# Mixer projections of a hybrid decoder: from one f32 product to three products of rounded parts

## The reference, cut to what matters

```
x += 1/2 * gate1 * SwiGLU(mod1(norm(x)))
h  = mod2(norm(x));  z = h @ W_in        # one projection for all mixer groups and branch gates
     A: u * (tril(W_s) v + b)            # spatial gating, columns ua, va
     B: forgetting attention, 8 heads    # qb, kb, vb, forget rows; paged cache for the samples
     C: mLSTM, 4 heads                   # qc, kc, vc, oc, input and forget rows
x += gate2 * W_out( sum_b sigmoid(g_b) * (y_b @ W_branch_b) )
x += 1/2 * gate3 * SwiGLU(mod3(norm(x)))
```

## Time and profile before

| | us |
|---|---|
| median of 3 runs | 3485.57 (3480.32 to 3488.34) |
| the profiled execution, its own time | 3474.84 |
| span of the profiled execution | 3473.1 |
| granted TensorE clock, mean | 0.971 |

### The profile page before, as it was taken

One profiled execution on the slowest core, in us unless ns is written; L12 is line 12 of the kernel. 1 busy time (PEld: TensorE's weight loads), 2 busy tenths in 40 slices (PEclk: granted clock), 3 DMA queues, 4 the chain that ended last, 5 costly groups with the idle time before them and its releaser, 6 DMA issues.

```text
span 3473.1 us, 49844 instructions
## 1 busy us (share of the span) xinstructions
PE 3302.7 (95%) x21518; PEld 2747.9 (79%) x21518; DVE 1053.2 (30%) x1901; ACT 705.1 (20%) x1072; POOL 138.0 (4%) x269
## 2 busy tenths in 40 slices
PE   6999999989899998999989999999898999989999
PEld 4999986656676687999979999865565767879999
DVE  3332340132531114333343333311334211143333
ACT  2221222120431002212122222121123210022121
POOL 0000000001102000000000000000021020000000
PEclk9999999989999999999999999999999999999999
DMA  5344431201228521232213333311021384112221
GB/s 225 146 156 169 153 120 50 85 25 34 90 79 279 178 103 57 114 138 105 110 73 139 153 146 128 129 74 61 25 72 57 118 272 158 73 73 86 85 89 72
DMA packets 115404, 390.53 MB, mean 112 GB/s; under 512 B 12416, under 2 KB 62944, under 8 KB 96880
## 3 DMA queue, kind: packets, MB, share of 16 engines
q1 hardware_dynamic: 97152, 338.36, 26.8%
q0 software_dynamic: 14432, 34.09, 2.8%
q10 hardware_dynamic: 3600, 14.89, 1.1%
HBM read 373.61 MB, written 13.69 MB: 112 GB/s over the span
## 4 chain that ended last, share of the span: by engine, by line
PE 85%; DVE 7%; DMA 4%; ACT 2%; SPq 1%; issue 1%; ACTq 0%; DVEq 0%
PE g L716 75%; PE tb L716 5%; PE q L716 4%; DMA w<-in_w_up 2%; DVE area L1933 2%; DMA area<-in_w_ada 1%; DMA area<-in_cache_v 1%; DVE area L1615 1%; DVE area L1845 1%; DVE w_lo L1658 1%; DVE h_lo L1627 1%; PE tb L719 1%; DVE area L1616 1%; ACT w_hi L1281 0%; DMA area<-in_cache_k 0%
## 5 line engine op out<-in xcount | busy, mean ns | idle before, releaser
L716 PE MATMUL g<-h_hi,w_hi 128*128 128x272 f32 x2816 | 590.4, 291 | 37.6 <-DVE h_lo L1627 24.7
L716 PE MATMUL g<-h,w 128*128 128x272 f32 x2304 | 570.1, 404 | 28.5 <-DVE area L1915 24.4
L716 PE MATMUL g<-h_lo,w_hi 128*128 128x272 f32 x2816 | 591.1, 291 | 0.0
L716 PE MATMUL g<-h_hi,w_lo 128*128 128x272 f32 x2816 | 584.5, 289 | 0.0
L716 PEld LDWEIGHTS g<-h,w 128*128 128x128 f32 x2304 | 443.1, 195 | 151.7 <-issue 32.7
L1281 ACT ACTIVATE w_hi<-w 128x1024 fp32r<-128x1024 f32 (+2 forms) x240 | 274.2, 1144 | 1262.7 <-PE g L716 935.8
L716 PEld LDWEIGHTS g<-h_hi,w_hi 128*128 128x128 f32 x2816 | 443.0, 190 | 59.5 <-ACT area L1295 27.7
L1658 DVE TENSOR_TENSOR w_lo<-w,w_hi 128x1024 fp32r<-128x1024 f32 (+2 forms) x240 | 319.3, 1332 | 509.7 <-ACT w_hi L1281 506.4
L716 PEld LDWEIGHTS g<-h_hi,w_lo 128*128 128x128 f32 x2816 | 448.5, 191 | 0.0
L716 PEld LDWEIGHTS g<-h_lo,w_hi 128*128 128x128 f32 x2816 | 447.0, 190 | 0.0
L716 PE MATMUL g<-area,w 128*128 128x272 f32 x1280 | 307.4, 395 | 3.4 <-DVE area L1919 2.6
(11 more groups left out here) (220 smaller groups left out, 2254.3 us busy)
## 6 DMA issues: line engine op xcount, KB each, us to landing
w<-in_w_up SPq DMA_DIRECT2D x44, 2048.0 KB, 8.1
w<-in_w_ada SPq DMA_DIRECT2D x32, 2048.0 KB, 8.2
w<-in_w_in SPq DMA_DIRECT2D x16, 2048.0 KB, 8.2
w<-in_w_down SPq DMA_DIRECT2D x16, 1536.0 KB, 7.3
w<-in_w_gate SPq DMA_DIRECT2D x48, 512.0 KB, 5.3
w<-in_w_down SPq DMA_DIRECT2D x16, 1280.0 KB, 5.8
area<-in_cache_k SPq DMA_DIRECT2D x72, 256.0 KB, 4.4
area<-in_cache_v SPq DMA_DIRECT2D x72, 256.0 KB, 4.2
```

Of the source, the lines that this page charges most:

```text
L716: return pe.matmul(o, a, b, start=start, stop=stop, skip_group_check=True, **kw)
```

## The change

The mixer's projections, the gate rows, the queries and keys and the branch gates become three products of rounded parts, as in the feed-forward. The branch products and the output product stay f32.

`norm` now splits the mixer's input too; the lower part `HX` lies in x's place. x is stored block by block as it comes ready, and loaded again in two halves after the last gate. Queries move to `YB`'s place and keys to a place of their own, `KB_`. Weights are split by pieces of 128x1024: 57 pieces a mixer, listed in `JOBS`. ACT rounds a piece into a place of `FIRST_HI`, `LATER_HI`, `VALUE_HI` or `WHM` (`hi_part`), DVE writes the lower part over the original in the slot (`lo_part`), and PE waits for the piece (`split_in`). Both are put by hand between the other steps of ACT's and DVE's programs; those of the fills hang on the half unit before (`next_job`).

Some waits move: the third page load of a layer (n == 2) waits for the sample scores and ACT's stores, the loads of the past forget values (POOL, line 684) for the end of vb, and the reload of x for the last gate.

```diff
+JOBS = [("ua", i) for i in range(4)] + [("va", i) for i in range(4)] + [("rows", 0)]
+JOBS += [(name, i) for name in ("qkc", "vc", "oc") for i in range(4)]
+JOBS += [("qk", i) for i in range(8)] + [("vb", i) for i in range(4)]
+JOBS += [("merge", i) for i in range(3 * KD)]
...
+def next_job(u):
+    what, _, h = FILLS[u]
+    kind, i = fill_job(u)
+    if h or what.startswith("branch") or (kind, i + 1) not in JOB:
+        return None
+    return kind, i + 1
...
                     if n == 2:
-                        sp.wait_ge(s_fd, 48 * l + 16)
+                        sp.wait_ge(s_ss, 2 * (l + 1))
+                        sp.wait_ge(s_outa, 16 * 11 * (l + 1))
...
-                        sp.wait_ge(s_ss, 2 * (l + 1))
-                        sp.wait_ge(s_outa, 16 * 11 * (l + 1))
-                        sp.wait_ge(s_xs, 16 * (l + 1))
-                        sp.dma_start(X[:], out["y"]).then_inc(s_xr, 16)
+                    if name == "out1":
+                        sp.wait_ge(s_xs, 128 * (l + 1))
+                        sp.wait_ge(s_fill, FILL_L * l + LAST_GATE + 1)
+                        for q in range(2):
+                            sp.dma_start(X[:, 4 * q:4 * q + 4, :], out["y"][:, 4 * q:4 * q + 4, :]).then_inc(s_xr[q], 16)
...
+            def split_in(l, job):
+                pe.wait_ge(s_ml, len(JOBS) * l + JOB[job] + 1)
+                return piece(l, job)[2:]
...
+            def thirds(o, hi, lo, k, h, begin, end):
+                cols = slice(h * HALF, (h + 1) * HALF)
+                for i, (w, x) in enumerate(((hi, HH), (hi, HX), (lo, HH))):
+                    last = mm(o, w, x[:, k, cols], begin and i == 0, end and i == 2)
+                return last
...
+            def project_tokens(l, name):
...
+                        for q, (x, w) in enumerate(((HH, hi), (HH, lo), (HX, hi))):
+                            last = mm(G[0:m, 2 * p, :], x[:, k, i * P:i * P + m], w, k + q == 0, k == KD - 1 and q == 2)
...
+            def hi_part(l, *jobs):
+                for job in jobs:
+                    name, raw, hi, _ = piece(l, job)
+                    if name:
+                        at = AT["mix", (l, name)]
+                        ac.wait_ge(s_w[at % 2], LANDED[at])
+                    ac.activation(hi, raw, ACT.Copy).then_inc(s_mh, 1)
...
                 squares()
+                ac.wait_ge(s_unit, un.u.value())
+                hi_part(l, ("ua", 0), ("ua", 1))
                 roots(3 * l + 1)
+                for k in range(KD):
+                    wait(t["tn"])
+                    ac.activation(HH[:, k, :], TN[:, k % 2, :], ACT.Copy).then_inc(s_hh, 1)
+                    if k in (5, 6):
+                        hi_part(l, ("ua", k - 3))
...
+            def lo_part(l, *jobs):
+                for job in jobs:
+                    _, raw, hi, lo = piece(l, job)
+                    ve.wait_ge(s_mh, split[0])
+                    ve.tensor_tensor(lo, raw, hi, ALU.subtract).then_inc(s_ml, 1)
...
+            def lo_fills(l, units):
+                for u in units:
+                    if next_job(u):
+                        lo_part(l, next_job(u))
```

More of the change, by code:

```diff
@@ L264, in build @@
         cst = sb("cst", [P, CONST_W])
+        w_at = top[0]
         W = [sb(f"w{i}", [P, SLOT]) for i in range(2)]
+        WR = [sb(f"w_rest{i}", [P, SLOT], F32R, over=w_at + 4 * SLOT * i) for i in range(2)]
+        x_at = top[0]
         X = sb("x", [P, KD, T])
+        HX = sb("h_rest", [P, KD, T], F32R, over=x_at)
         h_at = top[0]
@@ L274, in build @@
         GN = sb("gn", [P, L, 3 * KD])
+        pre_at = top[0]
         GVA = sb("gva", [P, 512])
@@ L278, in build @@
         WSS = sb("wss", [NS, 4, NS])
+        wfi_at = top[0]
+        WFI = sb("wfi", [P, KD, 44])
+        WFL = sb("wfi_lo", [P, KD, 44], F32R, over=wfi_at)
+        top[0] = pre_at + 4 * 2048
+        WHM = [sb(f"w_hi_fill{i}", [P, 1024], F32R, over=pre_at + 4096 * i) for i in range(2)]
         BROWS = sb("brows", [44, 1])
         GQK = sb("gqk", [P, 2])
-        WFI = sb("wfi", [P, KD, 44])
         M0 = sb("m0", [ROWS, SEQS])
@@ L353, in build @@
         VBLK, _ = take(2, SEQS, P, start=o_s)
-        PG, o_p = take(4, 512)
-        GATE = dict(a=take(T, start=o_p)[0], c=YS[:, 0, 0], b=YS[:, 0, 0])
+        KB_, o_p = take(4, T)
+        PG, _ = take(4, 512, start=o_p)
+        GATE = dict(c=YS[:, 0, 0], b=YS[:, 0, 0])
         ZT = YS[:, 0, 1]
@@ L866, in project @@
                 for b in range(0 if first is None else 2, blocks):
-                    product(unit(), [w[:, k, b * P:(b + 1) * P] for k in range(KD)], hk)
-            def project_tokens(l, i):
-                s = weights(l, i)
+                    p = unit()
+                    hi, lo = split_in(l, (name, b))
+                    for k in range(KD):
+                        for h in range(2):
+                            last = thirds(G[0:hi.shape[2], 2 * p + h, 0:HALF], hi[:, k, :], lo[:, k, :], k, h,
+                                          k == 0, k == KD - 1)
+                    last.then_inc(s_unit, 1)
+            def project_tokens(l, name):
                 for i in range(5):
@@ L929, in _ @@
                 wait(small, 9)
-                p = unit()
-                product(p, [WFI[:, k, :] for k in range(KD)], hk, m=44)
+                project(l, "rows", 1)
                 project(l, "qkc", 4)
@@ L1331, in f @@
                                                                                   dict(bias=ZERO[0:m, 0:1])))
-                each(5, f)
+                each(5, f, l, then)
             def read(l, units):
@@ L1556, in _ @@
                 ffn(l, 1)
-                wait(small, 9)
             ac.wait_ge(s_outa, outs.value())
@@ L1610, in norm @@
                     if k < KD:
-                        split = part != 1
-                        o = TN[:, k % 2, :] if split else H[:, k, :]
-                        if split and k >= 2:
+                        o = TN[:, k % 2, :]
+                        if k >= 2:
                             ve.wait_ge(s_h, hr.value())
@@ L1749, in _ @@
                 ffn(l, 0)
+                lo_part(l, ("ua", 0), ("ua", 1))
                 norm(3 * l + 1)
+                lo_part(l, ("ua", 2), ("ua", 3), *[("va", i) for i in range(4)], ("rows", 0))
                 wait(small, 9)
@@ L1755, in _ @@
                 un.take(9)
+                lo_part(l, *[("qkc", i) for i in range(4)])
                 for i in range(5):
@@ L1808, in _ @@
                     .then_inc(s_wrow, 1)
+                lo_part(l, *[("oc", i) for i in range(4)], ("qk", 0))
                 un.take(5 + 5 + 4)
@@ L1902, in _ @@
                 ve.sem_inc(s_stn, 1)
-                ve.sem_inc(s_lff, 1)
+                lo_fills(l, IN_MLSTM.early[20] + IN_MLSTM.late[20] + IN_MLSTM.early[21])
+                lo_part(l, *[("vb", i) for i in range(4)], ("merge", 0))
                 def read(units):
```

184 lines of the change are left out of this document (125 added, 59 removed).

## The result

| | before | after |
|---|---|---|
| median | 3484.69 us (3480.32 to 3488.34, 4 runs) | 3392.96 us (3389.73 to 3397.05, 4 runs) |
| ratio | | 0.9738, 95% interval 0.9721 to 0.9755 |
| profiled execution | 3474.84 us, clock 0.971 | 3397.05 us, clock 0.958 |

The change makes the kernel 91.7 us faster; 3380 was predicted, with 3340 to 3440 around it. One execution in this study, of the kernel with spread loads and moved pieces, ran slow (3624.11 us at a clock of 0.814) and is left out of that kernel's median.

What follows compares the result with a forecast made beforehand. TensorE, busy 95% of the span, was taken as the bound, so cheaper matmuls pay where others wait for it. Terms sum to -52.5 us a layer, -105 for two, from 3474.84 to 3370; 3380 us predicted as median, range 3340 to 3440.

Steps and rivals of the forecast that it cites:

- Price of a product: TensorE: three fp32r matmuls take 377 ns against 460 at 272 columns, 678 against 862 at 512 (226 each).
- Wide fp32r isn't cheap: Rival, token products: 512-column fp32r matmuls cost half of f32, 431 ns each; 3528 us, chance 0.03.
- Norm, ua, va, rows, qkc, vc and its open piece: Projections up to vc: norm and ua +2.3, va and vc -7.4 each, rows -1.3, vc's last piece +1.5 us a layer.
- oc and the first piece of queries: oc projection and after: cheaper units, but oc's last piece and the first of queries cost +1.1 us each on ACT.
- mLSTM and the 48 matmuls behind it: Shorter fills, less waits and pieces at head changes: -3 us a layer in the mLSTM, -3 behind it.
- rival of the half clock: Rival, mLSTM and prompt attention: idle PE stays at half clock, 0.69 instead of 0.46 us a matmul; 3496 us, chance 0.04.
- Norm of queries and keys, prompt attention: Before the sample scores: pieces ahead of roots and reciprocals cost +3.7, cheaper gate ticks give -6.6 us a layer.
- Sample attention: 128 cheaper gate matmuls partly lost to waits for pages: -5 us a layer (0 to -10.6).
- Last merge and x: 128 gate matmuls with PE as bound, -10.6 us a layer (-6 to -10.6); x's reload covered, costed at nothing.
- Fills that don't pay: Rival, mLSTM, attentions and merge: shorter fills only become longer waits, plain products alone gain; 3437 us, chance 0.13.
- Open pieces: Rival, hand-over from ACT to DVE to PE: all 57 pieces lie open, +48 us a layer; 3582 us, chance 0.06.

Runs made afterwards that it cites:

- spread loads and moved pieces: Changed kernel with merge weight loads issued between page quads and pieces moved in the mLSTM and three other places: 3363.99 us, 0.9670 of the kernel before.
- again: The changed kernel itself run and profiled a second time, nothing altered: 3392.65 us median of 5, 0.9750 of the kernel before.
- Without their pieces: Changed kernel with weight pieces of queries and keys left out from the third block on, gates' pieces still made: 3380.72 us, 0.9728 of the kernel before.
- fp32 fills: Changed kernel with queries, keys and branch gates back to one fp32 product, their 32 pieces per layer not made: 3417.92 us, 0.9812 of the kernel before.
- without pieces: Changed kernel with three-product fills reading two leftover weight buffers from the third block of queries on, no pieces made there: 3364.27 us, 0.9665 of the kernel before.
- the spread one: Changed kernel with only SP's issue order altered, page quads going between the merge weight loads: 3378.31 us, 0.9706 of the kernel before.

## Why the prediction was right, and where it was off

**Price of a product.** The 272-column matmul was read right (126 ns), the 512-column one 5 ns too low: 231, between the ends 215 and 237. "Wide fp32r isn't cheap" is out.

**Norm, ua, va, rows, qkc, vc and its open piece.** Forecast 2.3 - 7.4 - 1.3 - 5.3 - 7.4 + 1.5 = -17.6, measured 155.8 to 139.7 = -16.1, and 138.6, so -17.2, again. va and vc gave 6.6 us each, not 7.4; the norm with ua cost 1.5, not 2.3, which makes up for one of the two. The open piece stood where it was said to: DVE makes the last piece of vc ahead of the spatial gate's first drain, and PE waits 1.09 us for that drain.

```profile
602.65 1.23 DVE L1761 TENSOR_TENSOR w_rest<-w,w_hi_vc 128x1024 fp32r<-128x1024 f32 x1 [4.80 <-ACT w_hi_vc L1425]
603.91 0.69 DVE L1915 TENSOR_TENSOR area<-g,bs 128x512 f32<-128x512 f32 x1
```

```profile
604.76 1.67 PE L796 MATMUL g<-wst,area 128*128 128x128 f32 x8 [1.09 <-DVE area L1917]
```

**oc and the first piece of queries.** -4.2 forecast for oc (-5.3 for its units, +1.1 for its last piece), -4.7 measured in the first layer; 1.1 for the piece, and oc's end to the first mLSTM scores did go from 13.3 to 14.4 us.

**mLSTM and the 48 matmuls behind it.** -6 forecast, +1.1 in front; measured -2.4 / +0.2, and +0.1 / -2.8 again. The wait at a change of heads went from 4.05 to 4.46 us at the first one, but from 2.70 to 4.24 and 4.11 at the others: the forecast read one wait of the earlier trace rows and took it for all. That is 3.4 us of longer waits where 2.5 were costed. Without their pieces the stretch is 3 to 8 us shorter.

The larger miss is a term that the forecast has only as a rival: the clock. By the trace's record of the clock, PE is at its lower level, 1.2 GHz, for 37.5 us of this stretch in both layers before, and for 44.4 / 51.2 us after. Two layers of one execution do the same work, so they show the price: 143.2 and 145.8 us here, 151.1 and 144.0 with fp32 fills (51.2 and 34.1 us at the lower level), 131.9 and 137.7 without pieces (27.3 and 41.0). That is some 0.4 us for each us at the lower level. With that taken out, as an estimate, the stretch is 130.5 us before, 130.4 to 130.6 with fp32 fills, 125.0 to 125.4 in the two profiles of the changed kernel and 121.0 to 121.3 without pieces. So at an equal clock the stretch gains 5.1 to 5.5 us, where 4.9 were forecast with the piece in front; its pieces cost 4, and the lower clock takes 3 to 5 back. No run holds the clock still, so this share is worked out and not shown by an experiment. The rival of the half clock is partly here, then, though not for the whole stage, as it was put; by its own terms it also leads to 3501 us and not 3496.

**Norm of queries and keys, prompt attention.** -2.9 forecast, -1.6 / -1.4 measured. The run without pieces saves 7.4 / 9.9 us against before, as the -6.6 and the -2 of two faster ticks allow; the pieces take 6 to 8 back, where 5.6 (3 x 1.06 + 2 x 1.23) were costed. All is lost in the norm: the last 71.8 us of the prompt attention are 71.5 without pieces, so their cover there held, as forecast.

**Sample attention: the term that was mis-sized most.** -5 forecast. -0.6 measured in the first layer, +2.4 in the second. PE's own gain is larger than the 10.6 us given as the upper end: 144 of the gate matmuls lie in this stage, not 128, which is 12.0 us. The waits for pages grew from 4.9 to 11.8 us (13.3 again) and from 3.8 to 11.1, some 7 us a layer. What is left, 4 to 7 us, goes with the clock, which fell at each of these waits: 3.4 and 0 us at the lower level before, 13.7 and 17.1 after, at the same 0.4 us for each (an estimate, as above). The prediction named the cause, "faster ticks run into the same pages", and looked at the DMA engines' 82%. What the runs showed instead is SP's queue: four loads of merge weights, 4.8 us, ahead of a page. With them spread the waits are 8.3 and 6.5 us, the time at the lower level is 10.2 and 3.4 us, and the forecast for this and the last stage is met. The forecast had no term for the clock here.

**Last merge and x.** -10.6 forecast, -9.1 measured: 112 gate matmuls lie here, not 128, and 112 x 83 ns are 9.3 us. x's reload was not awaited: from the output product's start to the second feed-forward part's long stretch it is 163.0 us before and 162.8 after.

**The sum.** -52.5 a layer forecast; the profiles have -41.2 and -34.4, and -38.3 and -39.2 again, the medians -91.7 for both. The terms in front of the mLSTM and the values hold to within a fifth, and the fills paid 12.6 instead of 24.5 us. "Fills that don't pay" is refuted as a whole; in the mLSTM and the sample attention the fills paid, and longer waits and the lower clock took most of it back. "Open pieces" is refuted in the fills, the only place where all were taken away: 0.47 us apiece.

## What to carry to other kernels

When matmuls that fill another stage's waits become cheaper, look at the loads which that stage waits for, and at what stands ahead of them on the issuing queue: here more than half of a stage's gain came back by changing the order of issues alone. A preparation of 1.2 us per weight block is free beside a long run of matmuls and costs nearly its full time, 1.13 us, between the steps of an engine that sets the pace, so its place in the program matters more than its length. And a stage whose clock moves can hide a real gain of 3 us, or feign one, in a single profile; two profiles of one kernel, or two layers of one profile, show how far it moves by itself, and the granted clock beside each time tells the two apart. A wait costs more than its own length when the clock falls at it.

## What the runs showed of the hardware

The same DMA issue on SP, of one block of `w_branch`, takes from 0.65 to 4.36 us in the timelines of the merge step at 1038 to 1044 us: 0.65 for the first, 2.59 for the second in the changed kernel and, two issues behind a page's loads, 4.36 in the spread one:

```profile
1043.09 0.56 SPq L660 DMA_DIRECT2D w<-in_w_gate  x1
1043.69 4.36 SPq L662 DMA_DIRECT2D w<-in_w_branch  x1
```

What holds SP there no run isolates.

The granted clock fell to its lower level, 1.2 GHz, behind some waits and not behind others. In the mLSTM of the 14 profiles there are 84 waits at changes of heads. Behind all 48 of more than 4 us the clock fell, during the wait or up to 1.4 us after it; behind the 8 of 3.48 to 3.67 us it fell 7 times, and behind the 28 of 2.70 to 3.13 us 13 times. The Trainium skill (TensorE: Matmul & The Clock Gate, HAM oscillation) lays the lower clock to idle gaps between bursts of matmuls. The long waits here agree with that. What decides behind the short ones, and how much of the work behind a wait is hit, isn't settled here.
